# Quarters of the output weights requested by ScalarE, and a final norm per partition for the second token half

## The reference, cut to what matters

```
h = h + 0.5 * gt1 * swiglu(u, ffn1_w_in, ffn1_w_out)
h = h + gt2 * token_mixer(...)
h = h + 0.5 * gt3 * swiglu(u, ffn2_w_in, ffn2_w_out)
return rmsnorm(h, final_norm)      # h * rsqrt(mean(h*h) + 1e-6) * final_norm
swiglu(x, w_in, w_out) = (silu(x @ w_in[:, :F]) * (x @ w_in[:, F:])) @ w_out
```

## Time and profile before

| what | value |
|---|---|
| three runs, median (lowest, highest) | 2260.81 us (2259.23, 2266.37) |
| profiled execution, its time | 2263.8 us |
| its span | 2262.1 us |
| mean granted clock of TensorE | 0.987 |
| TensorE matmuls, busy | 2181.8 us (96%) |
| VectorE, ScalarE, GpSimd, busy | 1266.0, 817.0, 1286.4 us |
| DMA | 236.27 MB, 104 GB/s over the span |
| DMA queues in use for data | one, 31.9% of 16 engines' span |

### The profile page before, as it was taken

How to read it: one execution, slowest core, us unless ns; L and a number is a source line. 1 busy time by engine, 2 the same in 40 slices (tenths; PEclk the granted TensorE clock), 3 DMA queues, 4 the chain that set the end, 5 groups by cost and what they waited for, 6 DMA issues and landing times.

```text
span 2262.1 us, 27922 instructions
## 1 busy us (share of the span) xinstructions
PE 2181.8 (96%) x10289; PEld 1761.5 (78%) x10289; DVE 1266.0 (56%) x1971; ACT 817.0 (36%) x1513; POOL 1286.4 (57%) x1036
## 2 busy tenths in 40 slices
PE   7999999998999999999999999999999999999997
PEld 4688888886887777778777788888778888878886
DVE  6956666667857327656655202243955444458845
ACT  5522232233445314355545201023523333233444
POOL 5677878878854432312212233336778887768841
PEclk9999999999999999999999999999999999999999
DMA  9054454566333310011101113111053333364332
GB/s 345 28 168 154 152 159 139 169 233 215 94 102 113 103 47 1 11 29 38 29 28 31 45 47 121 47 47 47 24 174 115 112 98 112 98 257 147 99 98 103
DMA packets 222793, 236.27 MB, mean 104 GB/s; under 512 B 9775, under 2 KB 154306, under 8 KB 222402
## 3 DMA queue, kind: packets, MB, share of 16 engines
q1 hardware_dynamic: 222658, 234.49, 31.9%
HBM read 185.69 MB, written 48.76 MB: 104 GB/s over the span
## 4 chain that ended last, share of the span: by engine, by line
PE 77%; DVE 8%; ACT 4%; DMA 3%; issue 3%; POOL 2%; SPq 1%; DVEq 0%; ACTq 0%; POOLq 0%
PE ps L2371 30%; PE ps L2428 15%; PE ps L2242 13%; PE ps L2325 12%; POOL w_lo L987 1%; DMA x_raw<-hid_dram 1%; DVE h L2038 1%; DMA ada_full<-in_w_ada 1%; PE ps L2513 1%; PE ps L2623 1%; PE ps L2287 1%; DVE x_op L1818 1%; ACT h L1485 1%; PE ps L2588 1%; DVE h L2061 1%
## 5 line engine op out<-in xcount | busy, mean ns | idle before, releaser
L2428 PE MATMUL ps<-x_op,w_hi 128*128 128x512 f32 x1232 | 385.0, 394 | 13.5 <-DVE x_op L1818 13.5
L2371 PE MATMUL ps<-t,w_hi 128*128 128x512 f32 x1280 | 395.5, 390 | 1.1 <-POOL w_lo L987 1.0
L987 POOL TENSOR_TENSOR w_lo<-w_raw,w_hi 128x512 fp32r<-128x512 f32 x240 | 347.4, 1460 | 63.1 <-ACT w_hi L1241 63.1
L952 POOL TENSOR_SCALAR w_hi<-w_raw 128x1024 fp32r<-128x1024 f32 x55 | 57.8, 1050 | 471.3 <-PE ps L2242 295.7
L1241 ACT ACTIVATE w_hi<-w_raw 128x512 fp32r<-128x512 f32 x240 | 143.8, 626 | 414.7 <-DMA w_raw<-in_ffn_w_in 172.7
L2428 PEld LDWEIGHTS ps<-x_op,w_hi 128*128 128x128 f32 x1232 | 233.5, 190 | 65.1 <-issue 14.5
L2371 PEld LDWEIGHTS ps<-t,w_hi 128*128 128x128 f32 x1280 | 239.4, 188 | 52.3 <-POOL w_lo L987 2.4
L987 POOL TENSOR_TENSOR w_lo<-q,w_hi 128x512 fp32r<-128x512 f32 x132 | 193.2, 1468 | 125.4 <-ACT w_hi L1241 125.4
L2371 PE MATMUL ps<-t,w_lo 128*128 128x512 f32 x640 | 249.1, 389 | 0.0
L2428 PE MATMUL ps<-x_op,w_lo 128*128 128x512 f32 x616 | 241.6, 392 | 0.0
L1818 DVE TENSOR_TENSOR x_op<-x_raw,x_op 128x512 fp32r<-128x512 f32 x154 | 161.8, 1062 | 120.4 <-ACT x_op L1251 119.8
(11 more groups left out here) (292 smaller groups left out, 4271.8 us busy)
## 6 DMA issues: line engine op xcount, KB each, us to landing
w_raw<-in_ffn_w_in SPq DMA_DIRECT2D x88, 512.0 KB, 4.4
hid_dram<-hid_raw SPq DMA_DIRECT2D x154, 256.0 KB, 5.2
x_raw<-hid_dram SPq DMA_DIRECT2D x154, 256.0 KB, 2.6
ada_half<-in_w_ada SPq DMA_DIRECT2D x96, 256.0 KB, 3.2
w_raw<-in_w_in SPq DMA_DIRECT2D x41, 512.0 KB, 3.6
q<-in_ffn_w_out SPq DMA_DIRECT2D x6, 2816.0 KB, 12.2
ada_full<-in_w_ada SPq DMA_DIRECT2D x24, 512.0 KB, 11.4
x_tile<-in_x SPq DMA_DIRECT2D x8, 512.0 KB, 5.1
```

What stands on the lines that cost most here:

```text
L952: nc.gpsimd.tensor_scalar(w_hi[:, slot, :], w_raw[:, slot, :], 1.0, 0.0, ALU.mult, ALU.add).then_inc(w_high, 1)
L987: nc.gpsimd.tensor_tensor(lo, src, hi.bitcast(F32), ALU.subtract).then_inc(hs_ready, 1)
L2371: mm = nc.tensor.matmul(ps[bank][:], w[i], x[:, k, :], start=(first and k == 0 and q == 0), stop=(k == 3 and q == 2), skip_group_check=True)
L2428: mm = nc.tensor.matmul(ps[down_bank(p) + m][:], w[:, tile(m)], x_op[:, n % 3, x, :], start=(p in (0, 1, 3) and k == 0 and q == 0), stop=( ...
```

## The change

It has two parts.

**Requests.** All seven quarter requests of an FFN move from SyncE's queue to ScalarE's. In ScalarE's `fast_tile` of the last tile, behind the copies of blocks 0 to 2, stand the first three pieces of Q00; behind its second weight copy, Q10; in its `down`, at step 2, the last piece of Q00 and Q01, and at step 5, behind a wait for all stores of hidden blocks, Q11. SyncE keeps the activation blocks and stores: blocks 0 to 3, the last tile's five stores, blocks 4 to 8, the wait for the stores, blocks 9 on.

**Final norm of the second half.** TensorE transposes tiles 0 to 3 of its `h` before the root is known. The mean square of its tokens is made per partition (the sum of squares as the stationary operand, one column of ones as the moving one, into four columns of PSUM), Ln and Exp run on 128x4 (`rs_col`), and the root is multiplied in as a scale per partition when PSUM is evacuated. The gains go into tiles 0 to 3 by four VectorE products at steps 44 to 47, and into tiles 4 to 7 by diagonal matrices (`gain_diag`, made at steps 60 to 63), which take the place of the identity in the transposing product. ScalarE evacuates one half of each tile of the second token half, VectorE the other, and each half, 256 KB, is stored by itself.

```diff
--- SyncE
@@ def down(f):
                 for i in range(4):
                     hidden_in(f, i)
-                sp.wait_ge(hs_used, n + 2)
-                quarter_load(f, 6, q00[:, 2:4, :], 0, 0, 0, 2)
-                quarter_load(f, 0, q00[:, 4:10, :], 0, 0, 2, 8)
-                sp.wait_ge(hs_used, n + 3)
-                quarter_load(f, 1, q00[:, 0:2, :], 0, 0, 8, 10)
-                sp.wait_ge(hs_used, n + 5)
-                quarter_load(f, 3, q10[:], 1, 0, 0, PAIRS)
-                sp.wait_ge(hs_used, n + 7)
-                quarter_load(f, 2, q00[:, 10:11, :], 0, 0, 10, 11)
-                quarter_load(f, 4, q01[:], 0, 1, 0, PAIRS)
-                for i in range(4, 8):
+                hidden_out(f, LAST)
+                for i in range(4, 9):
                     hidden_in(f, i)
-                hidden_out(f, LAST)
-                hidden_in(f, 8)
                 sp.wait_ge(hid_out, 16 * (f + 1) * DOWN_STEPS)
-                quarter_load(f, 5, q11[:], 1, 1, 0, PAIRS)
                 for i in range(9, DOWN_STEPS):
                     hidden_in(f, i)
@@ the end
             for t in range(TT):
-                sp.wait_ge(o_ready, 8 * (t // 4) + 4 + t % 4 + 1)
-                sp.dma_start(out[0][t * P:(t + 1) * P, :], o_tile[t]).then_inc(o_stored, 16)
-            sp.wait_ge(o_stored, 16 * TT)
+                if t < 4:
+                    sp.wait_ge(o_ready, 4 + t + 1)
+                    sp.dma_start(out[0][t * P:(t + 1) * P, :], o_tile[t]).then_inc(o_stored, 16)
+                    continue
+                sp.wait_ge(o_ready, 4 + t + 1)
+                sp.dma_start(out[0][t * P:(t + 1) * P, half(0)], o_tile[t][:, half(0)]).then_inc(o_stored, 16)
+                sp.wait_ge(o_dve, t - 3)
+                sp.dma_start(out[0][t * P:(t + 1) * P, half(1)], o_tile[t][:, half(1)]).then_inc(o_stored, 16)
+            sp.wait_ge(o_stored, 16 * 12)
--- ScalarE
@@ def down(f):
                 for n in range(DOWN_STEPS):
+                    if n == 2:
+                        act.wait_ge(hs_used, tile_hs(f, LAST) + 7)
+                        quarter_load(f, 2, q00[:, 10:11, :], 0, 0, 10, 11)
+                        quarter_load(f, 4, q01[:], 0, 1, 0, PAIRS)
+                    if n == 5:
+                        act.wait_ge(hid_out, 16 * (f + 1) * DOWN_STEPS)
+                        quarter_load(f, 5, q11[:], 1, 1, 0, PAIRS)
                     if n >= 3:
                         x_highs(f, n)
@@ def fast_tile(f, t):
                     for i in range(3):
                         x_highs(f, i)
+                    act.wait_ge(hs_used, n + 3)
+                    quarter_load(f, 6, q00[:, 2:4, :], 0, 0, 0, 2)
+                    quarter_load(f, 0, q00[:, 4:10, :], 0, 0, 2, 8)
+                    quarter_load(f, 1, q00[:, 0:2, :], 0, 0, 8, 10)
                 act.wait_ge(tile_step, step(f, t, C11))
                 nc.scalar.activation(g1_b, g1_b, ACT.Silu).then_inc(silu_ready, 1)
                 high_hs(n + 10 if t < LAST else n + 7)
                 if t == LAST:
                     high_hs(n + 8)
+                if t == LAST:
+                    act.wait_ge(hs_used, n + 5)
+                    quarter_load(f, 3, q10[:], 1, 0, 0, PAIRS)
@@ the end
-            for i in range(2 * TT):
-                hf, kg, t = i // 8, i // 4 % 2, 4 * (i // 8) + i % 4
-                if i == 4:
-                    squares(3, 12, 14)
-                if i == 6:
-                    squares(3, 14, 16)
-                    root(3, 1)
+            for i in range(8):
+                kg, t = i // 4, i % 4
+                if i in (2, 3):
+                    squares(3, 8 + 2 * i, 10 + 2 * i)
                 act.wait_ge(y_t, i + 1)
-                nc.scalar.activation(o_tile[t][:, half(kg)], ps[i % 4 + 4 * hf][:], ACT.Copy).then_inc(o_ready, 1)
+                nc.scalar.activation(o_tile[t][:, half(kg)], ps[i][:], ACT.Copy).then_inc(o_ready, 1)
+            act.wait_ge(ms_done, 8)
+            nc.scalar.activation(rs_col[:], ps[7][:, 0:4], ACT.Ln, bias=eps_c[:, 0:1], scale=1.0 / D).then_inc(ln_ready, 1)
+            act.wait_ge(ln_ready, 8)
+            nc.scalar.activation(rs_col[:], rs_col[:], ACT.Exp, scale=-0.5).then_inc(rstd_ready, 1)
+            act.wait_ge(rstd_ready, 8)
+            for j in range(4):
+                act.wait_ge(y_t, 8 + j + 1)
+                nc.scalar.activation(o_tile[4 + j][:, half(0)], ps[j][:], ACT.Copy,
+                                     scale=rs_col[:, j:j + 1]).then_inc(o_ready, 1)
--- VectorE
@@ def down(f):
+                    if f == 1 and 44 <= n < 48:
+                        dve.wait_ge(sq_ready, sq_count(3, 1, n - 44))
+                        nc.vector.tensor_scalar(h[:, n - 44, half(1)], h[:, n - 44, half(1)], final_gain(n - 44), None,
+                                                ALU.mult).then_inc(y_ready, 1)
+                    if f == 1 and 60 <= n < 64:
+                        nc.vector.tensor_scalar(gain_diag[:, n - 60, :], ident[:], final_gain(4 + n - 60), None,
+                                                ALU.mult).then_inc(diag_ready, 1)
@@ the end
             dve.wait_ge(rstd_ready, 8)
-            for k in range(KT):
-                final_y(1, k)
+            for j in range(4):
+                dve.wait_ge(y_t, 12 + j + 1)
+                nc.vector.tensor_scalar(o_tile[4 + j][:, half(1)], ps[4 + j][:], rs_col[:, j:j + 1], None,
+                                        ALU.mult).then_inc(o_dve, 1)
--- TensorE
@@ the end
-            for i in range(2 * TT):
-                hf, kg, t = i // 8, i // 4 % 2, 4 * (i // 8) + i % 4
-                if i == 8:
-                    mean_square(3, 1)
+            for i in range(12):
+                kg, t = i // 4 % 2, 4 * (i // 8) + i % 4
                 if i % 4 == 0:
-                    pe.wait_ge(y_ready, 8 * hf + 4 * kg + 4)
-                if i >= 4:
-                    pe.wait_ge(o_ready, i - 3)
+                    pe.wait_ge(y_ready, (8, 12, 4)[i // 4])
+                if i == 4:
+                    pe.wait_ge(acc_done, 2 * READS)
+                if i >= 8:
+                    pe.wait_ge(o_ready, i - 7)
                 for k in range(4 * kg, 4 * kg + 4):
-                    mm = nc.tensor.transpose(ps[i % 4 + 4 * hf][:, tile(k - 4 * kg)], h[:, k, tile(t)], ident[:])
+                    mm = nc.tensor.transpose(ps[i % 8][:, tile(k - 4 * kg)], h[:, k, tile(t)], ident[:])
+                mm.then_inc(y_t, 1)
+            pe.wait_ge(o_ready, 8)
+            pe.wait_ge(sq_used, half_added(3, 1))
+            for j in range(4):
+                mm = nc.tensor.matmul(ps[7][:, j:j + 1], rstd[3][1][:, tile(j)], ones[:, 0:1], start=True, stop=True)
+            mm.then_inc(ms_done, 1)
+            pe.wait_ge(diag_ready, 4)
+            for j in range(4):
+                if j == 3:
+                    pe.wait_ge(ln_ready, 8)
+                for k in range(4):
+                    mm = nc.tensor.matmul(ps[4 + j][:, tile(k)], h[:, 4 + k, tile(4 + j)], gain_diag[:, k, :], start=True,
+                                          stop=True)
                 mm.then_inc(y_t, 1)
```

More of the change, by code:

```diff
@@ L102, in build_program @@
         heads2 = sb("heads2", [P, 2])
-        sb("pad", [P, 80])
+        rs_col = sb("rs_col", [P, 4])
+        sb("pad", [P, 76])
         h = sb("h", [P, KT, S])
@@ L155, in build_program @@
             s2_b = at(st_, "s2_b", [P, 4, HALF])
+        with stage() as st_:
+            at(st_, "pad_diag", [P, 64 * 1024 // 4])
+            gain_diag = at(st_, "gain_diag", [P, 4, P])
         with stage() as st_:
@@ L397, in build_program @@
         o_ready = sem("o_ready")
+        o_dve = sem("o_dve")
+        diag_ready = sem("diag_ready")
         o_stored = sem("o_stored")
@@ L767, in hidden_in @@
                 sp.dma_start(x_raw[:, n % 4, :], hid_dram[n // PAIRS, n % PAIRS]).then_inc(x_in[n % 4], 16)
-            def quarter_load(f, j, out_, half_m, odd, k0, k1):
-                rows = W_OUT[f].rearrange("(k two p) c -> two p k c", two=2, p=P)
-                sp.dma_start(out_, rows[odd][:, k0:k1, half_m * HALF:(half_m + 1) * HALF]).then_inc(quarter_in[j], 16)
             def down(f):
@@ L1241, in high_hs, with quarter_load @@
                 nc.scalar.activation(hs_place(n)[0], src, ACT.Copy).then_inc(wa_high, 1)
+            def quarter_load(f, j, out_, half_m, odd, k0, k1):
+                rows = W_OUT[f].rearrange("(k two p) c -> two p k c", two=2, p=P)
+                act.dma_start(out_, rows[odd][:, k0:k1, half_m * HALF:(half_m + 1) * HALF]).then_inc(quarter_in[j], 16)
             def x_highs(f, n):
@@ L1726, in adds, with final_gain, final_y @@
                     nc.vector.tensor_tensor(rstd[n][hf], rstd[n][hf], sq_b[n][c % 2], ALU.add).then_inc(sq_used, 1)
-            def final_y(hf, k):
-                g0 = ROWS["final_norm"][0] + k
-                nc.vector.scalar_tensor_tensor(h[:, k, half(hf)], h[:, k, half(hf)], vecT[:, g0:g0 + 1], rstd[3][hf],
```

(6 more changed lines are left out.)

## The result

| kernel | median (lowest, highest), runs | profiled run, its span |
|---|---|---|
| before, in the same session | 2261.29 us (2258.69, 2266.37), 15 | 2263.8, 2262.1 us |
| changed | 2266.22 us (2264.01, 2268.53), 15 | 2267.64, 2265.9 us |

Ratio 1.0020, 95% interval 1.0012 to 1.0028: **slower, by some 5 us**, where 1.2 us less was forecast. It lies 1.7 us above the range, which ended at 2264.5.

A forecast was written before the change was run, and what follows sets the result against it. Matmuls are 77% of the chain, so only TensorE's idle places count: tail -6.9, hand-overs +3.8 and +1.7, block 3's copies +0.2, sum -1.2 on the 2260.8 median: 2259.6 us; range 2251.5 to 2264.5.

The forecast's parts named there:

- the tail: From TensorE's last product to the end: new final norm and half stores end it at 2255.2, -6.9 us.
- The requests: Hand-overs to the down projection in both FFNs: fifth activation block later by +3.8 and +1.7 us, plus 0.2.
- When x4 lands: Hand-over step timing the fifth activation block (block 4) behind five stores: +3.8 us in the second FFN, +1.7 first.
- Their data can start at 2026.6: Second hand-over: data of the stores and block 4 start then (509.1 in the first), 0.8 us from request to data.
- The halves: Hand-over: Q01 and SyncE's queue share transfers equally, so 3.9 us of stores and block 4 take 7.8 us.
- Rival B: Hand-over: Q01 is served first, block 4 later by +4.3 and +3.8 us; in all +1.4, 2262.2 us; chance 0.17.
- The engines' part: Behind the last product at 2237.4: first store requested at 2243.4, last copy at 2250.0, all half stores requested by 2250.4.
- 2254.2; with the 0.95 us ...: End of the kernel: 4.2 MB of stores run 10.0 us from 2244.2 to 2254.2, plus 0.95 us gives 2255.2.
- rival D: Behind the last product: TensorE's clock is half, forecast + 1.4 = 2261.0 us; its chance is within the forecast's 0.52.
- The gain products: Last down projection, steps 44 to 47: four VectorE products cost 0, at most 0.9 us, tightest at step 46.
- ScalarE held by no request: Hand-over: ScalarE's copies of blocks 3 and 4 are not late through a request holding it; otherwise the prediction is wrong.
- slower by over 0.3%: Whole kernel: slower by more than the 6.8 us a measurement can tell from no change; chance 0.06.

The follow-up runs named there:

- aligned tail alone: Kernel before with only the change's final norm, stores and gain products, pad cut to 72 columns so later tensors keep their addresses: 2258.93 us, -2.4.
- best version: Changed kernel, blocks 4 to 7 ahead of the stores, store waits and Q11 later, gain products at steps 48 to 51; pad of 72 columns: 2244.62 us; shifted 2250.14.
- aligned change: Changed kernel with the pad behind rs_col cut from 76 to 72 columns, so later tensors lie where they lay before: 2264.36 us, +3.0.
- the single queue with a better order: Kernel before, blocks 4 to 6 requested ahead of Q10, block 7 behind Q01, store wait ahead of block 10, Q11 behind block 11: 2250.24 us, -12.4.
- two queues with it: Old tail, quarters requested by ScalarE, blocks 4 to 7 ahead of the stores, waits for the stores and Q11 later: 2248.01 us, -13.1 against the kernel before.

## Why the prediction was wrong

By size, the two terms that made the miss are the tail, forecast at -6.9 and worth -2.4 by itself, and a term that the sum didn't have, a shift of the tensors by 32 bytes. The requests were forecast at +5.7 and cost +4.8, although a step of their working was wrong. In the order of the working:

**The step that failed first** stands in the part on the change, "When x4 lands": "Their data can start at 2026.6". It took the 0.8 us from request to data from the tail, where no other queue was at work. Beside a full queue it is 3.6 us, in both hand-overs, and 3.5 to 3.7 us in all 16 of the eight traces with two queues at the full clock. The halves that follow are right: with data from 2032.5, 3.9 us of transfer at the half rate until Q01 is through at 2038.9, the rest alone and 1.4 us to the landing, the same working gives 2041.0; the trace has 2041.15.

In the first hand-over, on the time scale of before, the later start (2.8) and stores requested 0.6 us later than I had them make the missing 3.3 us in block 4's landing (+5.0, forecast +1.7). They count in full only because of a second slip: I had Q01 through alone at 515.1, from the requests of before, but ScalarE requests Q00 there 4.3 us later than SyncE did (495.52 for 490.19, less the 1.0 by which all lies later there), so that 2.3 MB of Q01 were left when the stores began and shared to the end. In the second the delay cost 2.8, an earlier last sum gave 1.1 back, and Q01 was through ahead of block 4: +5.0 for +3.8. What the whole down projections lost is less, 2.8 and 4.2 us: later small gaps of before (1.05 and 0.8 us in all) are gone, and outside the gaps the products took 0.7 to 1 us less, as much as they differ between any two runs. The requests alone cost +4.8 us on the chip for 5.7 forecast: with errors of both signs, this sum was not far off. Rival B's end, not its mechanism, was nearer the landings.

**The tail was sized too well**: -4.8 us with the shift undone (24.64 to 19.87 us behind the last product), for -6.9. The engines' part is as forecast: first store requested 5.9 us behind the last product, last copy some 13 us behind it. The last half store is requested at 2260.69, 14.9 us behind it and not 13, as SyncE needs some 0.7 us for each; the transfers are full until 2263 all the same. The term that failed is "2254.2; with the 0.95 us ...": the bulk of the 4.2 MB ends at 17.3 us by the trace for 16.8, but then one engine has some 2 us left, which the old tail's four last stores did not show. The full clock held until all of TensorE's work was done, so rival D was wrong. The Trainium skill (TensorE: Matmul & The Clock Gate, "Part 4: PE-mode transpose") says that the full clock does not engage for transposes. This trace shows only that it isn't lost in them: 1.00 all through the 48 transposes, reached by the products before. What speaks against the rule is the trace of before, where it rose under them (0.74 in 2254:2255, 1.00 behind it).

**The gain products** were not free: VectorE's timeline ahead of the third gap:

```profile
2155.45 2.71 DVE L1896 SCALAR_TENSOR_TENSOR h<-ps,gate_c,h 128x512 f32<-128x512 f32 x4
2158.08 0.47 DVE L1917 TENSOR_SCALAR h<-h,vecT 128x512 f32<-128x512 f32 x1
2158.47 0.68 DVE L1841 TENSOR_TENSOR x_op<-x_raw,x_op 128x512 fp32r<-128x512 f32 x1
2159.08 1.51 DVE L1917 TENSOR_SCALAR h<-h,vecT 128x512 f32<-128x512 f32 x1
```

Four reads of PSUM, then gain products of which one takes the long form, 1.51 us, and TensorE waits 0.76 us. I took the sums by the short form (0) and had 0.9 us as the bound. The aligned tail alone came out at -2.4 us with an interval from -5.0 to -0.9; -4.8 + 0.8 = -4.0 lies in it. With the gains at step 48 and on, the tail is worth 2248.01 - 2244.62 = 3.4 us by the medians, 4.4 against the kernel before of each set; the two profiled executions have 23.2 and 19.9 us behind the last product.

**The term that was missing** is the 32 bytes. I costed the edits by their instructions, and an allocation that issues none got no line. It costs 1.9 us in the change, 4.6 in the tail alone, 1.8 or 5.0 in the best version, and 3 to 7 by single runs in the kernel before. The sum with what was measured: requests +4.8 and aligned tail -2.4 make +2.4 for the +3.0 of the aligned change, each good to about 2 us; the shift's 1.9 is then simply what is left to +4.9. Whether the shift costs the change less than the others isn't settled, as the intervals overlap. Its first gaps hardly move with the rate (11.23 and 10.34 us shifted, 10.38 and 10.37 aligned), so they are set by the stores' request and the delay more than by the rate; whether that is all was not tried.

The Trainium skill has a rule that names it (DMA: Bandwidth & Descriptors, "How a descriptor splits into AXI transactions"): a descriptor whose start is no multiple of 256 bytes needs one more bus transaction. The page puts it for what is read; here most of the shifted tensors are written. The 32 and the 64 bytes agree with it, as both leave the multiple and both lower the rate alike; they would agree with a multiple of 128 or 512 as well. By the page's count of 32-byte beats a 2048-byte row would need 1 or 2 beats more than 64, by my estimate 1.6 or 3%; the runs show 5.4% for 2 KB rows and 2.1% where 4 KB rows are most of the load, for either shift. So the rule may tell when, not how much. Shifts by 128 or 256 bytes were not tried.

**What was right:** the diff doesn't do for block 4 what the queue split suggests (request order on SyncE), the halves, ScalarE held by no request, the second queue's 23 MB, the tail's new bound in the transfers. The warning that requests of another engine win nothing by themselves held too: the single queue with a better order gives 2250.24 us, two queues with it 2248.01. I gave slower by over 0.3% a chance of 0.06; the measured 0.2% is inside "within 0.3%", the time all the same above the range.

## What to carry to other kernels

Read every line of a diff for what it moves in memory: a small tensor can shift all large ones off the start that the transfers want, and the first stage with full transfers shows it in any two traces, ahead of all changed code. When a gap is a wait for one transfer, list the waits that stand behind it on every engine with their own end times before pricing the gain, and put no wait for a store ahead of work that doesn't need it; here that was 12 to 13 of the 17.5 us.

## What the runs showed of the hardware that was not expected

- SBUF tensors 32 or 64 bytes further on, off the multiples of 256 where they lay: 387 to 391 GB/s in place of 406 to 409 in 502:512, where rows are of 2 KB (394 in the aligned change), 409 to 412 in place of 419 to 421 in 15:25, where most of the load has rows of 4 KB. The second holds for all 10 kernels that were shifted and all 10 that weren't.
- A queue that has run empty and is asked for a transfer while another is at full rate moves nothing for 3.5 to 3.7 us, be it a store or a block (16 hand-overs of eight kernels); with the engines idle it was 0.8. At 409 GB/s it is 3.5 to 3.6 us and at 387 it is 3.6 to 3.7: by my estimate some 1.4 MB of the other queue each time. What causes it stays open. From then on both move the same number of packets (315 and 314 in 3 us).
- With 4.2 MB of stores requested within 9 us, about one engine of the 16 ends some 2 us behind the others (14 packets in 2264:2265), whether the last four tiles are stored in 256 KB or 512 KB.
